# A state space layer's group loop on VectorE: six turns of a register loop against six turns of straight code

## The chip, the cores and the metric

The kernel runs on one NeuronCore of a Trainium2 chip, as one program. The time is device microseconds of one execution; a kernel is judged by the median of several runs. The engines have their names of the profile: PE is the matrix engine (PEld its weight loads), DVE is VectorE, ACT ScalarE, POOL GpSimd, SP the queue that issues most transfers; a q behind a name (DVEq) is the engine's sequencer, which runs register instructions, branches and waits and leaves the engine itself idle.

## What is computed

One inference step of a two-layer decoder: a Mamba-2 state space layer and a dilated attention layer, each between two gated feed-forward halves, for one prompt of 512 tokens and 8 samples of 8 tokens, all with the same weights. The change lies in the state space mixer:

```python
def ssd_mixer(u, conv_state, ssm_state, w_in, conv_w, conv_b, dt_bias, a_log, d_skip, norm_g, w_out):
    proj = u @ w_in
    z, xbc, dt_raw = ...
    xpad = jnp.concatenate([conv_state.astype(xbc.dtype), xbc], axis=1)
    xc = conv_b + sum(xpad[:, k:k + l] * conv_w[k] for k in range(CONV_W))
    xc = jax.nn.silu(xc)
    ...
    y, h_last = ssd_chunked(xs, dt, a, bm, cm, h0)
    y = y + d_skip.astype(f32).reshape(SSD_GROUPS, SSD_HPG)[:, :, None] * xs.astype(f32)
    gz = (y.reshape(b, l, D_INNER) * jax.nn.silu(z.astype(f32))).reshape(b, l, SSD_GROUPS, D_INNER // SSD_GROUPS)
    gz = gz * lax.rsqrt(jnp.mean(gz * gz, axis=-1, keepdims=True) + EPS)
    gz = (gz.reshape(b, l, D_INNER) * norm_g.astype(f32)).astype(u.dtype)
    return gz @ w_out, new_conv, new_ssm
```

There are 8 groups of 4 heads. A group has four tiles of 128 features to convolve with 4 taps (two of x, one of B, one of C), two tiles of the gate z, chunks of 128 tokens for the scan, and its own slice of w_in and w_out.

## The kernel before

The engines are programmed one by one, each in the order in which its code stands, and wait for each other on counting semaphores. All 576 tokens stand along the free axis, features on the 128 partitions. Products are made of a high and a low part of each factor for exactness: ACT makes the high part of a block of weights (`wh`, line 953), POOL subtracts it from the raw weights to have the low part (`wl`, line 793), PE multiplies three times.

The state space layer goes by groups. Group 0 and group 7 are written out, groups 1 to 6 are one loop body on every engine (`Fori`, with the turn's number in a register). The text calls the loop's pass for group g turn g. In turn g, DVE finishes the convolution of group g, adds the output product of group g-1 to x eight times (`back`, line 2739), does the masks, decays and states of group g, and moves the projections of group g+1 out of PSUM, PE being busy with these projections meanwhile. The start of a DVE turn is:

```python
conv(g, 2, 0)        # first tap of tile 2
back(g - 1, 0)       # x tile 0 += output product
conv(g, 2, 1)        # second and third tap
for m in range(1, 4):
    back(g - 1, m)
```

A tap is one multiply-add on 128x600 elements of SBUF (line 2710); the next tap reads what it wrote, so DVE waits for its own semaphore `dve_self` between them (`step`, with the class `Steps`, lines 132 to 154). PE's output product of tile m + 1 waits for `so_evac`, which `back` raises, since its PSUM banks are free only then. At the end of a turn DVE scales by the reciprocal root (lines 2918, 2921), adds to the four parts of the samples' state tile `h0` (line 2888, signal `ss_evac`), evacuates the gate (2719) and makes the low part of the output's factor (2929). SP stores `h0` when `ss_evac` has counted (line 650) and, next in its queue, loads the second-next block of weights (line 576), which ACT and POOL then split.

In the loop every count that depends on the turn is a value made from registers: a wait for `self.base + self.n`, `so_mm` for `g * 6 + ...`, the address of a column `cw[:, one(g * 20 + ...)]`. In straight code all of these are constants in the instruction.

Of the kernel before, what the change touches and what calls it, by code (L numbers as in the profile page):

```python
# [13 lines left out]

# [1 line left out]

# [1 line left out]

# [19 lines left out]
HEADS, GROUPS, HPG, PD, NST = 32, 8, 4, 64, 128  # L40
# [24 lines left out]
U_LOOP = U_GRP + 4  # L65
U_TAIL = U_GRP + 8 * GROUPS - 4
# [55 lines left out]
TREE_SUMMED = {0: 0, 1: 1, 3: 2}  # L122
PLAIN_U = {1: 0, 4: 1}
NORM_OF_FFN = (0, 2, 3, 5)
SSD_DVE_STEPS = 15
QKV_ORDER = (2, 5, 8, 0, 1, 3, 4, 6, 7)
AHEAD = 3
TB, TW = 6, TOK // 6
# [3 lines left out]
class Steps:  # L132
# [1 line left out]

    def __init__(self, eng, sem):
        self.eng, self.sem, self.base, self.n = eng, sem, 0, 0

    def done(self, ins):
        ins.then_inc(self.sem, 1)  # L140
        self.n += 1

    def wait(self):
        self.eng.wait_ge(self.sem, self.base + self.n)

    @contextmanager
    def loop(self, first, last, per):

        start, self.n = self.n, 0
        with self.eng.Fori(first, last) as i:  # L150
            self.base = (i - first) * per + start
            yield i
        assert self.n == per, f"{self.n} signals in a turn, not {per}"
        self.base, self.n = 0, start + (last - first) * per

def step_kernel(nc, io):
    with ExitStack() as ctx:
# [241 lines left out]
        def two(ap):  # L400

            return ap.rearrange("p (h n) -> p h n", h=2)
# [1869 lines left out]
        def _(dve):  # L2272
            self_ = Steps(dve, dve_self)
# [362 lines left out]
            def ssd():  # L2636
# [92 lines left out]
                def back(g, m):  # L2729

                    if m % 4 == 3:
                        u = U_TAIL + 2 + m // 4 if isinstance(g, int) and g == GROUPS - 1 else None
                        if u is None:
                            u = U_TAIL + m // 4 if isinstance(g, int) else (g + 1) * 8 + (U_LOOP + 3 * (m // 4))
                        dve.wait_ge(unit_done, u + 1)
                    else:
                        dve.wait_ge(so_mm, g * 6 + (m - m // 4 + 1))
                    b = 2 * (m % 2)
                    V.tensor_tensor(two(x[:, m, :]), two(x[:, m, :]), ps[:, b:b + 2, 0:HALF], ALU.add).then_inc(so_evac, 1)

                def group(g, first, last):
# [8 lines left out]
                    if not first:  # L2750
                        conv(g, 2, 0)
                        back(g - 1, 0)
                        conv(g, 2, 1)
                        for m in range(1, 4):
                            back(g - 1, m)
# [7 lines left out]
                    if last:  # L2763
                        back(g - 1, 4)
                        back(g - 1, 5)
                    else:
                        conv(g, 3)
                        if not first:
                            ahead(0)
# [186 lines left out]
                gate_in(0, 1, U_GRP + 5)  # L2956
                conv(0, 2)
                group(0, True, False)
                with self_.loop(1, GROUPS - 1, SSD_DVE_STEPS) as g:
                    group(g, False, False)  # L2960
                group(GROUPS - 1, False, True)

# [171 lines left out]
            for m in (1, 2):  # L3134
                V.tensor_tensor(sqs[:, m, :], x[:, m, :], x[:, m, :], ALU.mult)
            ffn(0, 1)
            ssd()

            ffn(1, 3)
# [176 lines left out]
```

## Time and profile before

| | us |
|---|---|
| runs | 2452.45, 2455.61, 2458.88 |
| median | 2455.61 |
| profiled execution | 2457.03 |
| its span | 2455.2 |
| PE busy | 2413.4 (98% of the span) |
| DVE busy | 1854.5 (76%) |
| ACT busy | 1394.2 (57%) |
| POOL busy | 735.9 (30%) |
| mean granted clock of PE | 0.992 of full speed |
| DVE's loop of groups 1 to 6 | 494.9 to 893.5 of the span |

Busy time is of the engine's own instructions; register instructions, branches and waits are not in it. A timeline row gives the start of an instruction and its length; brackets behind it, where there are any, give the idle time of the engine ahead of it and what ended that. A row without brackets followed the one before it with no idle time that the view shows.

### The profile page before, as it was taken

How to read it: one execution, taken by the hardware profiler on the slowest of the kernel's cores; microseconds unless marked ns; L12 is line 12 of the kernel's file. 1: busy time of each engine (PE TensorE's matmuls, PEld its weight loads, DVE VectorE, ACT ScalarE, POOL GpSimd, SP SyncE). 2: the span in 40 equal slices, each digit the busy share in tenths (PEclk: the TensorE clock that was granted, in tenths of full speed). 3: DMA queues.
4: the chain of work that ended last, by engine and by line, in shares of the span. 5: the costliest groups of instructions: out<-in, count | busy, mean ns of one | idle time of the engine just before them, and what ended most of it. 6: DMA issues, size and time to landing. Idle time of an engine off the chain costs nothing.

```text
span 2455.2 us, 50197 instructions
## 1 busy us (share of the span) xinstructions
PE 2413.4 (98%) x19713; PEld 2361.6 (96%) x19713; DVE 1854.5 (76%) x3054; ACT 1394.2 (57%) x2388; POOL 735.9 (30%) x675
## 2 busy tenths in 40 slices
PE   8999999999999999999999999999999999999998
PEld 8999999899999989999999999999999998999998
DVE  8979767978888888978876988875235438988875
ACT  7757553645555556757666767664223227767663
POOL 1222233444445532222223122224322321222222
PEclk9999999999999999999999999999999999999999
DMA  7777743123333325677765677763443334677762
GB/s 192 165 169 174 164 121 113 47 95 106 106 106 97 105 82 132 165 162 169 166 146 133 155 173 161 172 148 129 158 133 123 136 110 105 161 171 162 174 149 89
DMA packets 105686, 339.01 MB, mean 138 GB/s; under 512 B 13776, under 2 KB 17360, under 8 KB 87184
## 3 DMA queue, kind: packets, MB, share of 16 engines
q1 hardware_dynamic: 53936, 242.40, 29.9%
q0 software_dynamic: 51552, 93.87, 22.7%
q8 instruction: 137, 2.24, 0.4%
q14 instruction: 61, 0.50, 0.1%
HBM read 223.06 MB, written 19.32 MB: 99 GB/s over the span
## 4 chain that ended last, share of the span: by engine, by line
PE 90%; DVE 6%; issue 2%; ACT 1%; DMA 1%; DVEq 0%; SPq 0%; POOL 0%; POOLq 0%; ACTq 0%
PE ps L1641 17%; PE ps L1639 17%; PE ps L1649 17%; PE ps L1537 6%; PE ps L1545 6%; PE ps L1538 6%; PE ps L1658 2%; PE ps L1659 2%; PE ps L1666 2%; PE ps L1977 1%; PE ps L1979 1%; PE ps L1978 1%; PE ps L1588 1%; PE ps L1578 1%; PE ps L1579 1%
## 5 line engine op out<-in xcount | busy, mean ns | idle before, releaser
L1641 PE MATMUL ps<-sb_ual,sb_hw 128*128 128x288 f32 x2240 | 612.5, 295 | 0.0
L1639 PE MATMUL ps<-sb_uah,sb_hw 128*128 128x288 f32 x2240 | 609.1, 295 | 0.4 <-ACT sb_hr L1029 0.2
L810 POOL DMA_DIRECT2D sb_lw<-sb_rawf x328 | 283.0, 868 | 959.2 <-ACT sb_lw L984 942.5
L1639 PEld LDWEIGHTS ps<-sb_uah,sb_hw 128*128 128x128 f32 x2240 | 420.8, 188 | 1.0 <-issue 0.8
L1641 PEld LDWEIGHTS ps<-sb_ual,sb_hw 128*128 128x128 f32 x2240 | 421.1, 188 | 0.0
L793 POOL TENSOR_TENSOR sb_wl<-sb_raw,sb_wh 128x1024 fp32r<-128x1024 f32 (+1 forms) x106 | 262.3, 2475 | 410.6 <-ACT sb_wh L953 385.8
L1649 PE MATMUL ps<-sb_uah,sb_lw 128*128 128x288 f32 x2240 | 384.3, 293 | 0.6 <-DMA sb_lw<-sb_rawf 0.6
L1537 PE MATMUL ps<-sb_uh,sb_wh 128*128 128x288 f32 x1360 | 374.2, 302 | 0.7 <-DVE sb_zs L2719 0.6
L1538 PE MATMUL ps<-sb_ul,sb_wh 128*128 128x288 f32 x1360 | 367.3, 297 | 0.0
L1649 PEld LDWEIGHTS ps<-sb_uah,sb_lw 128*128 128x128 f32 x2240 | 327.9, 188 | 1.3 <-DMA sb_lw<-sb_rawf 0.8
L1537 PEld LDWEIGHTS ps<-sb_uh,sb_wh 128*128 128x128 f32 x1360 | 256.1, 188 | 8.3 <-issue 5.3
L982 ACT CAST sb_hw<-sb_rawf 128x512 fp32r<-128x512 f32 x336 | 208.3, 620 | 87.5 <-PE ps L1649 72.2
L1538 PEld LDWEIGHTS ps<-sb_ul,sb_wh 128*128 128x128 f32 x1360 | 256.2, 188 | 0.5
L1641 PE MATMUL ps<-sb_hl,sb_hw 128*128 128x288 f32 x896 | 243.9, 295 | 0.0
L1639 PE MATMUL ps<-sb_hh,sb_hw 128*128 128x288 f32 x896 | 243.3, 293 | 0.0
L953 ACT CAST sb_wh<-sb_raw 128x1024 fp32r<-128x1024 f32 (+1 forms) x106 | 111.4, 1052 | 205.2 <-PE ps L1545 127.8
L984 ACT ACTIVATE sb_lw<-sb_rawf 128x512 fp32r<-128x512 f32 x328 | 207.1, 632 | 0.0
L2338 DVE TENSOR_TENSOR sb_lw<-sb_tw,sb_hw 128x1024 fp32r<-128x1024 f32 x112 | 137.1, 1224 | 92.2 <-ACT sb_hw L1019 88.0
L1545 PE MATMUL ps<-sb_uh,sb_wl 128*128 128x288 f32 x1360 | 195.4, 296 | 0.0
L1019 ACT CAST sb_hw<-sb_tw 128x1024 fp32r<-128x1024 f32 x112 | 117.9, 1053 | 122.8 <-PE ps L1649 122.8
L1545 PEld LDWEIGHTS ps<-sb_uh,sb_wl 128*128 128x128 f32 x1360 | 186.3, 189 | 0.8 <-issue 0.6
L1641 PEld LDWEIGHTS ps<-sb_hl,sb_hw 128*128 128x128 f32 x896 | 168.4, 188 | 0.0
(366 smaller groups left out, 5115.1 us busy)
## 6 DMA issues: line engine op xcount, KB each, us to landing
sb_lw<-sb_rawf POOLq DMA_DIRECT2D x358, 256.0 KB, 3.6
sb_rawf<-w_ffn_in SPq DMA_DIRECT2D x87, 1024.0 KB, 5.1
sb_rawf<-w_ffn_so SPq DMA_DIRECT2D x32, 1024.0 KB, 5.1
sb_raw<-w_ssd SPq DMA_DIRECT2D x64, 512.0 KB, 3.6
sb_raw<-w_att SPq DMA_DIRECT2D x40, 512.0 KB, 3.9
sb_rawf<-w_ffn_out SPq DMA_DIRECT2D x32, 384.0 KB, 3.0
sb_h<-state SPq DMA_DIRECT2D x8, 1024.0 KB, 5.0
ssm_sample<-sb_h SPq DMA_DIRECT2D x8, 1024.0 KB, 4.8
```

Source lines behind the costliest of these rows:

```text
L793: pool.tensor_tensor(wl[parity][:, 0:width], raw[:, parity, 0:width], wh[parity][:, 0:width].bitcast(F32), ALU.subtract).then_inc(wl_done, 1)
L810: pool.dma_start(slot(lw, p), rawf[:, s % 2, i * BL:(i + 1) * BL], accum_op=ALU.add).then_inc(ld_in[i], 16)
L982: nc.scalar.copy(slot(hw, p), src).then_inc(hd_done, 1)
L984: nc.scalar.activation(slot(lw, p), src, ACT.Copy, scale=-1.0).then_inc(nd_done, 1)
L1019: nc.scalar.copy(slot(hw, 7, 2), tw[:, 2 * BL:4 * BL]).then_inc(ht34_done, 1)
L1537: pe.matmul(ps[:, b, 0:n], w, rh[:, k, t0:t0 + n], start=first and k == 0, stop=False)
L1538: pe.matmul(ps[:, b, 0:n], w, rl[:, k, t0:t0 + n], start=False, stop=False)
L1545: ins = pe.matmul(ps[:, b, 0:n], w, rh[:, k, t0:t0 + n], start=False, stop=last and k == nk - 1)
L1639: pe.matmul(out, w[:, k * P:(k + 1) * P], high[k], start=begins and k == 0, stop=False, skip_group_check=True)
L1641: pe.matmul(out, w[:, k * P:(k + 1) * P], low[k], start=False, stop=False, skip_group_check=True)
L1649: ins = pe.matmul(out, v[:, k * P:(k + 1) * P], high[k], start=False, stop=k == 3, skip_group_check=True)
L2338: V.tensor_tensor(slot(lw, 7, 2), tw[:, 2 * BL:4 * BL], slot(hw, 7, 2).bitcast(F32), ALU.subtract).then_inc(lt34_done, 1)
```

## The change

The DVE program alone is changed. The loop over groups 1 to 6 becomes a Python `for`, which writes six copies of the body one after the other with constants in all counts and addresses. The helper `loop` of `Steps` goes, with its base and the number of signals in a turn; `back` computes the same numbers for its waits in another form. PE, ACT, POOL and SP keep their loops with registers.

```diff
@@ class Steps
     def __init__(self, eng, sem):
-        self.eng, self.sem, self.base, self.n = eng, sem, 0, 0
+        self.eng, self.sem, self.n = eng, sem, 0
...
     def wait(self):
-        self.eng.wait_ge(self.sem, self.base + self.n)
-
-    @contextmanager
-    def loop(self, first, last, per):
-
-        start, self.n = self.n, 0
-        with self.eng.Fori(first, last) as i:
-            self.base = (i - first) * per + start
-            yield i
-        assert self.n == per, f"{self.n} signals in a turn, not {per}"
-        self.base, self.n = 0, start + (last - first) * per
+        self.eng.wait_ge(self.sem, self.n)
...
                 def back(g, m):
 
                     if m % 4 == 3:
-                        u = U_TAIL + 2 + m // 4 if isinstance(g, int) and g == GROUPS - 1 else None
-                        if u is None:
-                            u = U_TAIL + m // 4 if isinstance(g, int) else (g + 1) * 8 + (U_LOOP + 3 * (m // 4))
+                        u = (U_TAIL + 2 + m // 4 if g == GROUPS - 1 else U_TAIL + m // 4 if g == GROUPS - 2
+                             else (g + 1) * 8 + (U_LOOP + 3 * (m // 4)))
                         dve.wait_ge(unit_done, u + 1)
...
                 group(0, True, False)
-                with self_.loop(1, GROUPS - 1, SSD_DVE_STEPS) as g:
+                for g in range(1, GROUPS - 1):
                     group(g, False, False)
                 group(GROUPS - 1, False, True)
```

The listings show each engine's instructions in their order; lines of the changed kernel stand 11 or 12 lower. ISA and REGISTER_ALU are register work of the sequencer. The loop body of before has 66 such rows; in the changed kernel there are none, and DVE's listing grows from 2434 to 2759 rows. The listings of the other four engines have the same rows in the same order as before.

DVE at the start of a turn, before: the taps of tile 2 (`sb_acc`) around the first add to x.

```order
L2710 ISA [waits tap_done]
L2710 SCALAR_TENSOR_TENSOR sb_acc<-sb_xp,sb_cw,sb_acc 128x600
L144 ISA
L2737 ISA [waits dve_self]
L2739 TENSOR_TENSOR sb_x<-sb_x,ps 128x576 [waits so_mm]
L2710 ISA
L2710 SCALAR_TENSOR_TENSOR sb_acc<-sb_xp,sb_cw,sb_acc 128x600
L144 REGISTER_ALU
L2710 ISA [waits dve_self]
L2710 SCALAR_TENSOR_TENSOR sb_acc<-sb_xp,sb_cw,sb_acc 128x600
L2737 REGISTER_ALU
L2739 TENSOR_TENSOR sb_x<-sb_x,ps 128x576 [waits so_mm]
```

The same place of the changed kernel:

```order
L2699 SCALAR_TENSOR_TENSOR sb_acc<-sb_xp,sb_cw,sb_acc 128x600 [waits tap_done]
L2727 TENSOR_TENSOR sb_x<-sb_x,ps 128x576 [waits so_mm,dve_self]
L2699 SCALAR_TENSOR_TENSOR sb_acc<-sb_xp,sb_cw,sb_acc 128x600
L2699 SCALAR_TENSOR_TENSOR sb_acc<-sb_xp,sb_cw,sb_acc 128x600 [waits dve_self]
L2727 TENSOR_TENSOR sb_x<-sb_x,ps 128x576 [waits so_mm] x2
```

The engine's instructions and their waits are the same; the register rows between them are gone, and a wait that stood on a register row now stands on the instruction itself.

DVE at the normalization near the end of a turn, before: reciprocal, the two scalings (`sb_ysb`), the state update (`sb_h`).

```order
L2918 RECIPROCAL sb_gnr<-sb_gnr 128x576 [waits gz_ready,gsqrt_ready]
L144 REGISTER_ALU
L2921 REGISTER_ALU [waits dve_self]
L2921 SCALAR_TENSOR_TENSOR sb_ysb<-sb_ysb,sb_ng,sb_gnr 128x576
L2921 REGISTER_ALU
L2921 SCALAR_TENSOR_TENSOR sb_ysb<-sb_ysb,sb_ng,sb_gnr 128x576
L2887 REGISTER_ALU [waits ss_mm]
L2888 TENSOR_TENSOR sb_h<-sb_h,ps 128x512 [waits hm_done]
```

And in the changed kernel:

```order
L2906 RECIPROCAL sb_gnr<-sb_gnr 128x576 [waits gz_ready,gsqrt_ready]
L2909 SCALAR_TENSOR_TENSOR sb_ysb<-sb_ysb,sb_ng,sb_gnr 128x576 [waits dve_self]
L2909 SCALAR_TENSOR_TENSOR sb_ysb<-sb_ysb,sb_ng,sb_gnr 128x576
L2876 TENSOR_TENSOR sb_h<-sb_h,ps 128x512 [waits hm_done,ss_mm]
L2876 TENSOR_TENSOR sb_h<-sb_h,ps 128x512 [waits hm_done] x3
```

Here too the order of the engine's work stays, and the register rows behind the wait for `dve_self` are gone.

## Rows read from the trace of the kernel before

**Rows 1.** The page: its part 1, engines, and its part 4, the chain that ended last.

```profile
PE 2413.4 (98%) x19713; PEld 2361.6 (96%) x19713; DVE 1854.5 (76%) x3054; ACT 1394.2 (57%) x2388; POOL 735.9 (30%) x675
...
PE 90%; DVE 6%; issue 2%; ACT 1%; DMA 1%; DVEq 0%; SPq 0%; POOL 0%; POOLq 0%; ACTq 0%
```

**Rows 2.** Waits of PE in 494.9 to 893.5: engine, line, releaser, us, times, longest.

```profile
PE ps L1778 <- DVE sb_h L2888: 3.5, 1, 3.5
...
PE ps L1977 <- DVE sb_x L2739: 2.3, 1, 2.3
```

**Rows 3.** Chain of waits from 640 to 850: start us, us, what.

```profile
707.00 2.11 PE ps L1545 x16
...
775.84 2.13 PE ps L1545 x16
...
841.01 2.11 PE ps L1545 x16
```

**Rows 4.** Timeline of PE in turn 5: start us, us, engine, line, operation, idle before.

```profile
767.75 0.40 PE L1977 MATMUL ps<-sb_gh,sb_wh 128*128 128x288 f32 x1 [2.33 <-DVE sb_x L2739]
...
768.39 0.29 PE L1978 MATMUL ps<-sb_gl,sb_wh 128*128 128x288 f32 x1
...
768.92 0.44 PE L1978 MATMUL ps<-sb_gl,sb_wh 128*128 128x288 f32 x1
```

**Rows 5.** Timeline of DVE in turn 5, the add and the third tap.

```profile
762.42 0.75 DVE L2739 TENSOR_TENSOR sb_x<-sb_x,ps 128x576 f32<-128x576 f32 x1
...
764.07 2.97 DVE L2710 SCALAR_TENSOR_TENSOR sb_acc<-sb_xp,sb_cw,sb_acc 128x600 f32<-128x600 f32 x1
```

**Rows 6.** Timeline of POOL in turns 3, 4, 5 and the last group.

```profile
633.74 3.06 POOL L793 TENSOR_TENSOR sb_wl<-sb_raw,sb_wh 128x1024 fp32r<-128x1024 f32 x1 [4.54 <-ACT sb_wh L953]
...
698.92 2.98 POOL L793 TENSOR_TENSOR sb_wl<-sb_raw,sb_wh 128x1024 fp32r<-128x1024 f32 x1 [4.87 <-ACT sb_wh L953]
...
764.03 2.37 POOL L793 TENSOR_TENSOR sb_wl<-sb_raw,sb_wh 128x1024 fp32r<-128x1024 f32 x1 [4.45 <-ACT sb_wh L953]
...
897.87 2.37 POOL L793 TENSOR_TENSOR sb_wl<-sb_raw,sb_wh 128x1024 fp32r<-128x1024 f32 x1 [4.84 <-ACT sb_wh L953]
```

**Rows 7.** Timeline of DVE in turns 3, 4 and the last group.

```profile
633.69 0.85 DVE L2710 SCALAR_TENSOR_TENSOR sb_acc<-sb_xp,sb_cw,sb_acc 128x600 f32<-128x600 f32 x1
...
697.14 0.75 DVE L2739 TENSOR_TENSOR sb_x<-sb_x,ps 128x576 f32<-128x576 f32 x1 [0.39 <-PE ps L1979]
...
698.80 0.84 DVE L2710 SCALAR_TENSOR_TENSOR sb_acc<-sb_xp,sb_cw,sb_acc 128x600 f32<-128x600 f32 x1
...
896.34 0.75 DVE L2739 TENSOR_TENSOR sb_x<-sb_x,ps 128x576 f32<-128x576 f32 x1 [0.61 <-PE ps L1979]
...
897.88 3.00 DVE L2710 SCALAR_TENSOR_TENSOR sb_acc<-sb_xp,sb_cw,sb_acc 128x600 f32<-128x600 f32 x1
```

**Rows 8.** Timeline of DVE: reciprocal and line 2921, group 0 and turn 5.

```profile
486.73 3.74 DVE L2918 RECIPROCAL sb_gnr<-sb_gnr 128x576 f32<-128x576 f32 x1
...
490.51 2.68 DVE L2921 SCALAR_TENSOR_TENSOR sb_ysb<-sb_ysb,sb_ng,sb_gnr 128x576 f32<-128x576 f32 x1
...
817.65 3.75 DVE L2918 RECIPROCAL sb_gnr<-sb_gnr 128x576 f32<-128x576 f32 x1 [1.31 <-ACT sb_gnr L1358]
...
821.53 1.55 DVE L2921 SCALAR_TENSOR_TENSOR sb_ysb<-sb_ysb,sb_ng,sb_gnr 128x576 f32<-128x576 f32 x2
```

**Rows 9.** Line 2710 alone: engine, operation, count, ns min/median/max, first and last start.

```profile
L2710 DVEq FUSED_REGOPS  x72: 57/57/81, 495.0 to 868.1; - x72
```

**Rows 10.** Timeline of DVE, the first tap of turn 6.

```profile
830.06 0.83 DVE L2710 SCALAR_TENSOR_TENSOR sb_acc<-sb_xp,sb_cw,sb_acc 128x600 f32<-128x600 f32 x1
```

**Rows 11.** Timeline of DVE, the last state update of turn 4.

```profile
755.89 0.68 DVE L2888 TENSOR_TENSOR sb_h<-sb_h,ps 128x512 f32<-128x512 f32 x1
```

**Rows 12.** Timeline of SP, the transfer of the weights that follow.

```profile
757.37 0.35 SPq L576 DMA_DIRECT2D sb_raw<-w_ssd  x1
```

**Rows 13.** Waits of DVE in 494.9 to 893.5.

```profile
DVE sb_x L2739 <- PE ps L1979: 23.6, 34, 2.0
```

More of the change, by code:

```diff
@@ L17 @@
-from contextlib import ExitStack, contextmanager
+from contextlib import ExitStack
 import numpy as np
@@ L124 @@
 NORM_OF_FFN = (0, 2, 3, 5)
-SSD_DVE_STEPS = 15
 QKV_ORDER = (2, 5, 8, 0, 1, 3, 4, 6, 7)
```

## The prediction

> **What bounds the kernel now.** I read the page first: the matmul engine PE is busy 98% of the span and carries 90% of the chain that ended last [rows 1]. An edit on VectorE (DVE) can therefore pay only where PE waits for it. The loop of groups 1 to 6 lies between 494.9 and 893.5 us. The waits of PE in that stretch are two only: 3.5 us at its entrance and 2.3 us at line 1977 [rows 2]. The first has its cause in group 0, which is straight code already. It ends with the update of the state tile (line 2888) of group 0, which comes late since the scaling at line 2921 ran from 490.51 for 2.68 us. The later pair of the same operation took 1.55 us for both [rows 8]. The change does not touch that. So at most the second wait is to be had, and I looked at what it costs. In the chain of waits the same sixteen matmuls of the next group begin at 707.00, 775.84 and 841.01 [rows 3]: periods of 68.84 and 65.17 us. 
>
> **Why turn 5 and no other.** PE at 767.75 waits for an output tile to be added to x (line 2739), and that add stands behind the third tap of the convolution of tile 2 (line 2710, the second half of conv(g, 2)). This tap took 2.97 us in turn 5, from 764.07, and 0.84 us in the others [rows 5, 7]. GpSimd (POOL) started its subtraction of the low weights (line 793) at 764.03 [rows 6], 0.04 us ahead of it; it ends at 766.40, and the tap right after. In turn 3 the tap began at 633.69 and the subtraction at 633.74 [rows 6, 7]; there the tap took its 0.85 us, and the subtraction 3.06 us instead of 2.37. So these two shut each other out: whichever starts first keeps its pace, the other waits to its end. The tap is first by 0.05 us in turn 3 and 0.12 in turn 4; the rows of turns 2 and 6 read the same, with leads between these. It loses by 0.04 in turn 5, and by 0.01 in the last group, outside the loop [rows 5 to 7]. Only a tap that loses stops PE.
>
> The Trainium skill says this of the hardware: SBUF — State Buffer, section Who interferes with whom, has the port pair of the two engines as an exclusive lock, given by issue order, for the whole instruction. The trace agrees with it in both orders, as just read. By a shared bandwidth instead, 0.1 us of lead would be worth about 0.1 us a turn and the change nothing.
>
> **The change, part by part.** *The register work goes.* A turn of the loop has 66 register rows in the listing of DVE, the two of the loop's end among them; 72 of one line take 57 ns each [rows 9]. Most run while the engine is busy. They cost where DVE waits for its own last result and only then computes the next address. There the listing shows one ahead of each tap. From the start of the add at 697.14 to the third tap at 698.80 are 1.66 us in turn 4; the same three instructions in the last group, straight code, take from 896.34 to 897.88, 1.54 us [rows 7]. So a tap comes 0.11 or 0.12 us earlier after the add; I take 0.11. The add itself cannot come earlier than PE's output (line 1979): in turn 4 it waited 0.39 us for it. In turn 5 it did not wait, 762.42, while PE's event by the period of 65.1 us was due at 697.14 + 65.1 = 762.3; without the register rows in front of it the add comes at about 762.3.
>
> *What else moves.* The rival of the tap starts when its weights have landed, and SP issues that transfer at 757.37, behind a store that waits for the end of DVE's state update (line 2888, the last from 755.89 for 0.68 us) [rows 11, 12]. From the end of that update to POOL's start are 764.03 - 756.57 = 7.46 us. So POOL moves with DVE. Ahead of that update lies one gap with register work in it: from the reciprocal (817.65 + 3.75) to line 2921 at 821.53 are 0.13 us in the loop; in group 0 from 486.73 + 3.74 to 490.51 they are 0.04 [rows 8]. POOL comes 0.09 us earlier. The start of the reciprocal hangs on ScalarE and PE (idle 1.31 us before it) and stays.
>
> *The race after the change*, turn 5: tap at 762.3 + 1.54 = 763.84, POOL at 764.03 - 0.09 = 763.94. The tap leads by 0.10. In the others the lead changes by +0.11 - 0.09 where the add waits for PE: turn 4, 0.14. In turn 3 PE's event was due at 697.14 - 65.1 = 632.0; with it the tap comes at 633.54 and POOL at 633.65, a lead of 0.11. Turns 2 and 6 lie between. The last group was straight before; its POOL comes 0.09 earlier as well, so it loses by 0.10 and keeps its stall. Worth: -3.7 us in turn 5, 0 elsewhere.
>
> *The other DVE gaps* (some 0.1 us each, at the taps, the state recurrence and line 2726) end in waits for PE: 23.6 us for line 1979 alone over the six turns [rows 13]. They cost nothing now and give nothing. Bounds for all of it: 0, and the 57 ns of 66 rows in six turns, 22.6 us, were DVE the bound. With that waiting left on DVE, and PE idle in two places only, I take 0.
>
> *The end of the loop.* The trace shows no pause there: the first tap of turn 6, at 830.06, has no idle time ahead of it [rows 10]. Nothing is won. The Trainium skill, Runtime: NRT & Kernel Launch, section Instruction fetch mechanics, says that a taken branch to a page no longer held must wait for a fetch, which is why kernels prefer full unrolling. The trace does not agree for this loop: no idle time at its end, so by measurement this is worth 0 and not a fetch per turn.
>
> *The code grows* by five turns. A fetch that is late is not in this trace, so bounds: below, one register instruction's 57 ns won in each turn, 0.3 us; above, a stall as long as that of turn 5, 2.1 us on DVE in each of the five added turns. That would cost PE something only where it hits the stretch between 829 and 833 or its like. The straight last group, with the same instructions, shows no idle time but for PE. I take 0.
>
> **Sum.** The profiled execution took 2457.03 us (span 2455.2 and 1.8 around it). 2457.03 - 3.7 = 2453.3. It lies 1.4 us above the median shown, 2455.61; the three runs are 3.2 us apart each, about the size of one such stall, so a run seems to lose this race a varying number of times, and I set 2453.3 as the time, 0.1% under the median.
>
> **Rivals.**
> 1. *The race stays open.* Leads of 0.09 to 0.14 us are won against a landing whose delay differs between turns: POOL waited 4.45 us for its weights in turn 5 and 4.87 in turn 4 [rows 6]. One turn loses as before: 2457.0. For it: the tap lost by 0.04 only. Against: both sides hang on the same chain of DVE and PE, and the new leads are double the old.
> 2. *POOL wins (slower).* The state update moves earlier than the tap does. It decides from 0.2 us on: if POOL came 0.2 us earlier instead of 0.09, the leads of all five turns from 2 to 6 would be gone, as in the last group, where SP and POOL are out of their loops too. Five turns lost instead of one: 2457.0 + 4 x 3.7 = 2471.8; three lost: 2464.4. Against: between reciprocal and update I find the one gap.
> 3. *The last group too.* If its landing is late by 0.1 us, its tap wins, and PE's idle time behind it goes too: 2453.3 - 3.7 = 2449.6. Against: it goes the wrong way by the 0.09.
> 4. *DVE was the bound*, hidden behind matmuls whose ends are modelled: up to 22.6 us less; with half of it 2445.7. Against: a period of 65.1 us in every undisturbed turn, whether or not DVE stalled elsewhere in it.
> 5. *Nothing comes of it*, with other collisions of these two engines shifted by 0.1 us: counted with rival 1, the same time.
>
> **Chances.** Forecast 0.60, rival 1 (with 5) 0.23, rival 2 0.07, rival 3 0.07, rival 4 0.03. Changes of under 0.3% (7.4 us) can hardly be told from none with this kernel. Faster than 2448.2 needs rival 4 or rival 3 with luck: 0.05. Slower than 2463.0 needs rival 2 with three turns or more: 0.06. Within: 0.89. The range takes in rivals 1 and 3 and a microsecond or two of scatter as between the runs before: 2449.5 to 2459.0.
>
> **What would show it.** In the profile after: no register instructions on DVE; 1.54 us from add to third tap in each turn; the tap at 0.84 us in turns 2 to 6, and each of POOL's subtractions beside it near 3.0 us, not 2.37; the reciprocal's end to line 2921 in 0.04 us; no wait of PE for line 2739 in the loop; periods of 65.1 us throughout; the stall of the last group still there, and the 3.5 us at the loop's entrance. I am wrong in the mechanism if a turn has 65.1 us although its tap lost, or if PE's turns become shorter than 65.1; in the step on POOL if the time from the state update to its start is no longer near 7.46 us.

## The result, and the profile after

The changed kernel takes 2468.95 us (median of 16 runs, 2455.86 to 2473.39), the kernel before on the same chip 2459.45 us (median of 16, 2452.45 to 2464.76). The ratio is 1.003 with a 95% interval of 1.0019 to 1.0041: slower by 0.2 to 0.4%. The forecast was 2453.3 us in a range of 2449.5 to 2459.0, a change too small to be told from none. The profiled execution took 2461.54 us (span 2459.7), against 2457.03 before.

The page of the kernel after, its parts 1 and 4, reads almost as that of before [rows 1]:

```profile
PE 2412.9 (98%) x19713; PEld 2359.7 (96%) x19713; DVE 1865.0 (76%) x3054; ACT 1393.0 (57%) x2388; POOL 732.0 (30%) x675
...
PE 91%; DVE 6%; ACT 1%; issue 1%; DMA 0%; SPq 0%; POOL 0%; DVEq 0%; ACTq 0%
```

DVE is busy 10.5 us longer, with the same 3054 instructions. Some 6.6 us of that are three more taps that took 3.0 us instead of 0.84: time in which it is shut out. Three instructions of line 2817 (2829 before) also take some 2 us longer each, in turns 2, 3 and 6. PE does not wait for these: its periods there (below) are longer by the wait behind the tap alone. The waits of PE between 490 and 930 us say where it stands still (engine, tile, line, releaser: us in all, times, longest). This window takes in the last group, which that of [rows 2] leaves out:

```profile
PE ps L1966 <- DVE sb_x L2727: 10.9, 5, 2.2
PE ps L1767 <- DVE sb_h L2876: 3.6, 1, 3.6
```

Line 1966 is the old 1977, 2727 the old 2739, 2699 the old 2710. The one stall of the loop has become four, and the last group kept its own. In the chain of waits the same sixteen matmuls in turns 2 to 6 are these, where [rows 3] shows three of them (start us, us, what):

```profile
579.47 2.11 PE ps L1534 x16
...
646.75 2.11 PE ps L1534 x16
...
711.82 2.11 PE ps L1534 x16
...
780.61 2.12 PE ps L1534 x16
...
847.91 2.11 PE ps L1534 x16
```

The periods are 67.28, 65.07, 68.79 and 67.30 us. Only the second, with turn 4's tap in it, is undisturbed. The timelines of DVE and of POOL in turn 5, which answer to [rows 5] and [rows 6]:

```profile
767.13 0.76 DVE L2727 TENSOR_TENSOR sb_x<-sb_x,ps 128x576 f32<-128x576 f32 x1 [0.19 <-PE ps L1968]
767.80 3.91 DVE L2699 SCALAR_TENSOR_TENSOR sb_acc<-sb_xp,sb_cw,sb_acc 128x600 f32<-128x600 f32 x2
```

```profile
768.70 2.37 POOL L782 TENSOR_TENSOR sb_wl<-sb_raw,sb_wh 128x1024 fp32r<-128x1024 f32 x1 [4.47 <-ACT sb_wh L942]
```

The row of DVE holds two taps. The first keeps its 0.88 us to the next start, so the third started at 768.68 and ran 3.03 us. POOL started 0.02 us *behind* it and yet kept its 2.37 us. The turn was lost with the tap in front. Turns 2, 3 and 6 read the same, with leads of the tap of 0.03, 0.00 and 0.03 us (a lead is the time from the start of the third tap to the start of POOL's low weights). Turn 4 has a lead of 0.05 (its third tap starts at 703.61) and is won: both taps together take 1.72 us, and POOL is the one that is long.

```profile
702.06 0.76 DVE L2727 TENSOR_TENSOR sb_x<-sb_x,ps 128x576 f32<-128x576 f32 x1 [0.21 <-PE ps L1968]
702.74 1.72 DVE L2699 SCALAR_TENSOR_TENSOR sb_acc<-sb_xp,sb_cw,sb_acc 128x600 f32<-128x600 f32 x2
```

```profile
703.66 3.05 POOL L782 TENSOR_TENSOR sb_wl<-sb_raw,sb_wh 128x1024 fp32r<-128x1024 f32 x1 [4.51 <-ACT sb_wh L942]
```

**Why the leads are small.** The add waits for PE's last matmul of the tile (line 1968, line 1979 before). The timeline of PE, first of the kernel after in turn 5, then of the kernel before in turn 4:

```profile
766.73 0.30 PE L1968 MATMUL ps<-sb_gh,sb_wl 128*128 128x288 f32 x1
```

```profile
696.81 0.30 PE L1979 MATMUL ps<-sb_gh,sb_wl 128*128 128x288 f32 x1
```

It ends at 767.03 after, and the add starts at 767.13, 0.10 us later. It ended at 697.11 before, and the add started at 697.14 [rows 7], 0.03 us later. So in straight code the add itself reacts 0.07 us more slowly to the same event. What DVE's sequencer does at that add's waits (line, engine, operation, count in the whole program, ns min/median/max, first and last start), first in the kernel after, then in the kernel before:

```profile
L2725 DVEq EVENT_SEMAPHORE  x7: 21/21/21, 502.4 to 903.1; - x7
```

```profile
L2737 DVEq FUSED_REGOPS  x6: 53/53/53, 499.8 to 830.9; - x6
L2737 DVEq EVENT_SEMAPHORE  x1: 21/21/21, 896.3 to 896.3; - x1
```

The add has to wait twice: for the first tap of DVE itself and for PE. In the loop one register instruction of line 2737 stood between tap and add in each turn (53 ns, six of them for six turns), and the wait for the tap sat on it; the add carried PE's alone. In straight code nothing stands there. A semaphore instruction of its own takes one of the two waits, seven times after, and before only in the last group.

The register instruction had a price of its own when the tap ahead ended late. In turn 5 before, the first tap ended at 762.28, behind PE's last matmul, and the add started 0.14 us after the tap, 0.20 behind PE:

```profile
761.45 0.83 DVE L2710 SCALAR_TENSOR_TENSOR sb_acc<-sb_xp,sb_cw,sb_acc 128x600 f32<-128x600 f32 x1
```

This is how the loop lost that turn. In the kernel after the add is 0.11 us behind PE in every turn, also in turn 6, where the first tap ended with PE's matmul: the change made the latest add earlier and all the others later.

### The profile page after: what moved, and what is told of

It is laid out like the page before. It is cut to its first block, busy times and chain, and to the rows that moved or that the text cites. A ratio compares the mean times of both kernels' runs of the same rounds, so it can differ in the third digit from the quotient of the medians.

```text
span 2459.7 us, 49830 instructions
## 1 busy us (share of the span) xinstructions
PE 2412.9 (98%) x19713; PEld 2359.7 (96%) x19713; DVE 1865.0 (76%) x3054; ACT 1393.0 (57%) x2388; POOL 732.0 (30%) x675
## 4 chain that ended last, share of the span: by engine, by line
PE 91%; DVE 6%; ACT 1%; issue 1%; DMA 0%; SPq 0%; POOL 0%; DVEq 0%; ACTq 0%
PE ps L1630 17%; PE ps L1628 16%; PE ps L1638 16%; PE ps L1526 7%; PE ps L1534 7%; PE ps L1527 7%; PE ps L1647 2%; PE ps L1648 2%; PE ps L1655 2%; PE ps L1966 1%; PE ps L1968 1%; PE ps L1967 1%; DVE sb_acc L2699 1%; PE ps L1577 1%; PE ps L1567 1%; PE ps L1568 1%
```

## The experiments

Each group of kernels that ran together shared its runs of the kernel before.

**1. flat_free_add.** The second wait is taken off the add, and stands on the next tap:

```diff
-                        if t < CONV - 1:
+                        if part == 0 and k == 2:
+                            self_.done(ins)
+                        elif t < CONV - 1:
...
                         back(g - 1, 0)
+                        self_.wait()
                         conv(g, 2, 1)
```

> The changed kernel, with DVE's wait for its own first tap put behind the add to x that follows instead of ahead of it (the add doesn't read the tap). Race theory: the add then begins when PE's output is there, at 5.76 us behind the state update instead of 5.84, the third tap at 7.30, POOL at 7.41 to 7.43: a lead of 0.11 or more, the tap wins in turns 2 to 6; the last group, whose add already waits for PE, still loses. 8 to 13 us less than the changed kernel, ratio to before 0.997 to 1.000. Fetch theory: as the changed kernel, 1.003.

Measured: 2454.98 us, 0.9987 of before (0.9978 to 0.9996). Straight as the change, and yet faster than before. The timelines of PE, DVE and POOL in turn 5:

```profile
763.10 0.30 PE L1968 MATMUL ps<-sb_gh,sb_wl 128*128 128x288 f32 x1
```

```profile
763.43 0.76 DVE L2729 TENSOR_TENSOR sb_x<-sb_x,ps 128x576 f32<-128x576 f32 x1 [0.19 <-PE ps L1968]
764.11 1.72 DVE L2699 SCALAR_TENSOR_TENSOR sb_acc<-sb_xp,sb_cw,sb_acc 128x600 f32<-128x600 f32 x2
```

```profile
765.10 2.98 POOL L782 TENSOR_TENSOR sb_wl<-sb_raw,sb_wh 128x1024 fp32r<-128x1024 f32 x1 [4.56 <-ACT sb_wh L942]
```

The add comes 0.03 us behind PE again, the leads are 0.08 to 0.12 us in turns 2 to 6 and 0.10 in the last group, and no tap is lost. These are nearly the leads that the prediction gave (0.10 to 0.14). One wait moved by one instruction is the whole difference to the changed kernel. The last group had been expected to lose, and that it won is owed in part to chance: POOL started there 7.46 us behind the end of the state updates, against 7.26 to 7.29 in the profiles of the kernels before and after. With the same edit on the loop (experiment 7) it was 7.28, and the tap lost.

**2. flat_pool_late.** The changed kernel, with POOL made late instead: `pool.tensor_tensor(spare[:, 0:1], masks[:, 0:1], masks[:, 1:2], ALU.subtract)` in front of its first low weights of each turn.

> The changed kernel (straight code on DVE), with one tiny subtraction of POOL (128x1) ahead of its first low-weights subtraction of each turn, so that POOL comes some 0.1 to 0.2 us later to the third tap. Race theory (the tap lost in four turns of five because it leads by only 0.00 to 0.03 us): the leads become 0.1 us and more, the tap takes 0.84 us in turns 2 to 6 and perhaps in the last group too (it loses there by 0.06), PE has no 2.2 us wait in the loop; 10 to 15 us less than the changed kernel, some 2 to 8 us less than the kernel before: ratio to before 0.997 to 0.999. Fetch theory (straight code costs DVE or PE instruction loads): nothing in the code's length changes, ratio to before stays 1.003 to 1.004.

Measured: 2455.61 us, 0.9986 (0.9977 to 0.9995). The leads are 0.14 to 0.86 us in the loop, nothing is lost there, and 0.02 in the last group, which is lost. So the add may stay late, if only POOL is later. A lead of 0.85 us is the tap's whole length: there the tiny subtraction itself was shut out, and took up to 0.82 us instead of 0.19, after which the large one met no tap at all. POOL in turn 5 of flat_free_late (experiment 8), where the tap began at 768.35:

```profile
768.45 0.79 POOL L783 TENSOR_TENSOR sb_spare<-sb_masks 128x1 f32<-128x1 f32 x1 [4.76 <-ACT sb_wh L944]
769.20 2.39 POOL L784 TENSOR_TENSOR sb_wl<-sb_raw,sb_wh 128x1024 fp32r<-128x1024 f32 x1
```

**3. flat_reorder.** The changed kernel, with the adds that PE waits for ahead of the third tap: tap 1, add 0, tap 2, add 1, tap 3, add 2, add 3 (conv is cut into three parts for it).

```diff
                         back(g - 1, 0)
                         conv(g, 2, 1)
+                        back(g - 1, 1)
+                        conv(g, 2, 2)
-                        for m in range(1, 4):
+                        for m in range(2, 4):
```

> The changed kernel, with the second add to x moved ahead of the third tap (tap, add, tap, add, tap, add, add). The add reads PSUM and one tile of SBUF and was never held by POOL. Race theory: POOL now always starts before the third tap and holds it for up to 2.4 us in every turn, but PE needs only the second add at that time, so its 2.2 us waits for line 2739 go in all turns and in the last group: 12 to 18 us less than the changed kernel, ratio to before 0.995 to 0.998. If a held tap cost by itself (DVE behind for the rest of the turn), nothing would be won: 1.003. Fetch theory: 1.003 too.

Measured: 2456.10 us, 0.9988 (0.9979 to 0.9997), short of the 0.995 to 0.998 expected. The third tap is held in every turn, as here in turn 5, and costs PE no 2.2 us, since the add that PE waits for is already done:

```profile
765.92 2.36 DVE L2699 SCALAR_TENSOR_TENSOR sb_acc<-sb_xp,sb_cw,sb_acc 128x600 f32<-128x600 f32 x1
```

No wait of line 1966 for the add is left, but each turn pays some: periods of 65.29 to 65.33 us, since PE now waits elsewhere:

```profile
PE ps L1526 <- DVE sb_x L2727: 2.6, 6, 0.5
```

**4. loop_tap_late.** From the other side, the loop of before made to lose by a later third tap: `V.tensor_copy(spare[:, 0:1], masks[:, 0:1])` in front of it.

> The kernel before, loop and registers kept, with one tiny copy of DVE (128x1) ahead of the third tap, so that the tap comes some 0.1 us later. Race theory: the leads of 0.05 to 0.12 us are used up, the tap loses in most of turns 2 to 6, and each loss costs 2.2 us, or 3.7 us where the granted clock falls after it: 6 to 14 us more than the kernel before, ratio 1.002 to 1.006, as slow as straight code without being straight. Fetch theory: ratio 1.000.

Measured: 2457.49 us, 1.0001 (0.9991 to 1.0010). The expectation failed, since the tap was hardly delayed: from add to tap are 1.66 us instead of 1.65, the register work in front of the tap having run beside the copy. Leads 0.08 to 0.14 us in turns 2 to 6, none lost in the loop. It tells nothing of the race but that leads of this size win.

**5. loop_tap_later.** The same with three copies.

> The kernel before, loop kept, with three tiny copies of DVE (128x1) ahead of the third tap. One copy had moved the tap by 0.01 us only, since the register work ran beside it; three should move it by 0.15 to 0.25. Race theory: the leads of 0.05 to 0.12 us turn negative, the tap loses in all of turns 2 to 6, each at 2.2 us or, where the granted clock falls, 3.7: 8 to 16 us more than the kernel before, ratio 1.003 to 1.006. Fetch theory: ratio 1.000.

Measured: 2469.28 us, 1.0038 (1.0021 to 1.0055), as slow as the changed kernel, with the loop kept. So the loss needs no straight code. From add to tap 1.74 us; leads in turns 2 to 6 0.01, -0.03, 0.03, -0.02 and 0.00; four of these lost, and the last group. Its waits of PE:

```profile
PE ps L1977 <- DVE sb_x L2742: 11.4, 5, 2.3
```

It has the one turn in all profiles that was won with a lead under 0.04 us, turn 4. DVE and POOL there:

```profile
706.66 0.83 DVE L2713 SCALAR_TENSOR_TENSOR sb_acc<-sb_xp,sb_cw,sb_acc 128x600 f32<-128x600 f32 x1
```

```profile
706.68 3.06 POOL L793 TENSOR_TENSOR sb_wl<-sb_raw,sb_wh 128x1024 fp32r<-128x1024 f32 x1 [4.64 <-ACT sb_wh L953]
```

**6. flat_again.** The changed kernel once more, for a second profile.

> The changed kernel itself once more, beside the others of this call on one chip. Both theories: ratio to before 1.002 to 1.004. Race theory: three to five of turns 2 to 6 lose the third tap, with leads of 0.00 to 0.05 us, the add to x starts 0.11 us after the end of PE's last product for it (0.04 in the loop), and each lost turn shows one PE wait of 2.2 us.

Measured: 2464.34 us, 1.0019 (1.0007 to 1.0031). Leads 0.03, 0.05, 0.01, 0.01 and 0.04 us in turns 2 to 6. Again only the 0.05 is won; it is in turn 3 here, not in turn 4. The add is 0.11 us behind PE throughout. From the matmuls behind the output product in turn 1 to the same in the last group, six periods with all these races in them, 404.3 us pass, as in the first profile of this kernel (404.4), and against 398.1 and 397.2 in the two profiles of the kernel before. That its span is 10.7 us longer (2470.4) comes from elsewhere in the program.

**7. loop_free_add.** The edit of flat_free_add on the loop.

> The kernel before, loop kept, with DVE's wait for its own first tap put behind the first add to x. Race theory: turns in which the first tap ended late (as turn 5 before) now begin the add as soon as PE is done, 0.04 us after it; leads 0.09 to 0.12 in all five turns, none lost; the last group, straight code, gets its add 0.07 us earlier and wins about every second time. 3 to 6 us less than before, ratio 0.998 to 0.999, the same as straight code with the same edit (0.9987): then straight code by itself is worth less than 1 us. If straight code itself were worth something, or cost something, the two would differ.

Measured: 2459.39 us, 1.0002 (0.9991 to 1.0013). The profile is as expected in the loop (leads 0.07 to 0.10 us, all won, periods 65.11 to 65.17), and the last group was lost with 0.02. The time is not: it should have won 3.7 us wherever the kernel before loses a turn. Expected were 0.998 to 0.999. Either that kernel mostly loses none in runs without a profile, or the scatter hid it. This stays open.

**8. flat_free_late.** Both remedies on the changed kernel, **and 9. flat_late_again,** the same word for word beside its twin below.

> Both edits on the changed kernel: the wait for its own first tap behind the add, and POOL's tiny subtraction ahead of its large one. Race theory: leads of 0.2 us and more, no tap lost in any turn or the last group, in all runs: as the single edits or up to 2 us less, ratio 0.998 to 0.9987, with less scatter between runs. If the runs scatter as before, the scatter has another cause than this race.

> flat_free_late word for word, beside its loop twin. Both theories: ratio to the kernel before 0.998 to 0.999 as at its first run (0.9985), no third tap lost, periods of 64.9 to 65.05 us. Race theory: 0.0002 to 0.0003 under loop_free_late, which a timing of five rounds can hardly tell; rival: 0.0008 or more above it.

Measured: 2454.87 us, 0.9985 (0.9976 to 0.9994), then 2454.97 us, 0.9983 (0.9974 to 0.9993). Nothing lost, leads 0.19 to 0.86 us. Its runs still spread over 9 to 10 us, so most of the scatter is not the race. Some of it may be: the runs of the kernels that lose four or five taps in a profile spread over 18 us (the change), 13 (flat_again) and 20 (loop_tap_later).

**10. loop_free_late.** Both remedies on the loop of before. With the race out of both (here too no tap is lost, with leads of 0.18 to 1.24 us), this pair is the change by itself.

> Kernel before (turns as a loop) with both edits: the wait for DVE's own first tap stands behind the add, and POOL does one 128x1 subtraction ahead of its first low weights of each turn. The race is then out in the loop too, and what is left between this kernel and its straight twin flat_late_again is the worth of straight code by itself. Race theory: leads of 0.8 us or more in every turn and the last group, third tap 0.84 us, no PE idle at line 1977's place; periods of 65.10 to 65.15 us against 65.00 to 65.03 of the twin, so the twin is faster by 6 x 0.1 = 0.6 us, 0.0002 to 0.0003; ratio to the kernel before 0.998 to 0.999. Rival (straight code costs something outside this race, late instruction fetches for instance): this kernel is faster than its twin by 2 us or more.

Measured: 2454.03 us, 0.9978 (0.9966 to 0.9991); the straight twin 0.9983. The two can't be told apart. The straight twin's median is 0.9 us higher, and with twelve runs each, spread over 8 to 9 us, the true difference may be anything from 1 us in its favour to 3 us against it (an estimate from that spread). So the timing makes the rival, late instruction fetches of 2 us or more, unlikely and does not exclude it; the two profiles show no sign of it, the straight one being the shorter by 1.7 us (2453.2 against 2454.9). In the chain of waits straight code does have its 0.1 us a turn. First the loop, then the straight twin, the two sixteens around turn 5's output row:

```profile
760.85 2.13 PE ps L1547 x16
775.80 2.11 PE ps L1547 x16
```

```profile
759.29 2.11 PE ps L1536 x16
774.10 2.11 PE ps L1536 x16
```

14.95 us against 14.81. The periods are 65.11 to 65.17 against 64.99 to 65.05 us.

**11. flat_states_first.** flat_free_late, and in group 0 the state updates that the 3.5 us wait at the loop's entrance hangs on go ahead of the scalings:

```diff
+                    if first:
+                        sample_states(range(4))
                     for i in range(2):
                         V.scalar_tensor_tensor(two(ysb[:, i, :]), two(ysb[:, i, :]), ng[:, one(g * 2 + i)], inverse,
...
-                        sample_states(range(4))
+                        if not first:
+                            sample_states(range(4))
```

> flat_free_late, and in group 0 alone DVE does the four state updates ahead of the two scalings, not behind them. In flat_free_late the updates of group 0 come behind 3.4 us of scalings and PE waits 3.5 us for them at the entrance of turn 1, with a fall of the clock. If that wait ends last there: it goes, 3.5 us and up to 1.4 us of clock less, ratio 0.9985 - 0.0014 to 0.0020 = 0.9965 to 0.9971. Rival: the scalings come 2.5 us later, PE's next wait is for the output row (the halves of the gated row) instead, and the time stays at 0.9985 or gets longer by 1 to 2 us.

Measured: 2452.18 us, 0.9976 (0.9965 to 0.9986), the fastest of all, though not certainly faster than its parent (0.9983), and short of what was expected. Its waits of PE:

```profile
PE ps L1968 <- DVE sb_x L2731: 2.0, 1, 2.0
PE ps L1968 <- DVE sb_gl L2925: 1.5, 1, 1.5
```

The wait of 3.5 us went; 1.5 us came back at the output row, for the reason of the rival, and 2.0 us since everything in turn 1 had moved, and its third tap, which had never been near POOL, now met it with a lead of -0.02 us and took 2.99 us.

**12. before_again.** The kernel before, for a second profile.

> The kernel before word for word, for a second profile of it. Race theory: the add 0.03 to 0.05 us behind PE's event, leads of -0.05 to 0.13 us in turns 2 to 6, each turn with a lead of 0.04 us or less lost and each with 0.05 or more won, so none to two lost, and the last group lost. Rival (the order is settled by something else than these leads): turns lost at leads over 0.06.

Measured: 2458.06 us. Leads 0.01, 0.09, 0.12, 0.10 and 0.05 us in turns 2 to 6. Turn 2 is lost, the others won. DVE and POOL in turn 2:

```profile
569.46 4.01 DVE L2710 SCALAR_TENSOR_TENSOR sb_acc<-sb_xp,sb_cw,sb_acc 128x600 f32<-128x600 f32 x2
```

```profile
570.45 2.38 POOL L793 TENSOR_TENSOR sb_wl<-sb_raw,sb_wh 128x1024 fp32r<-128x1024 f32 x1 [4.51 <-ACT sb_wh L953]
```

Here the third tap begins at 570.44. So turn 5 was nothing special: the loop loses about one turn, now this, now that.

**All meetings together.** In the eleven profiles whose DVE has no copies and the old order there are 77 pairs of a third tap and low weights, the wide leads of turn 1 counted. The 17 lost taps have leads from -0.10 to 0.035 us; the 60 won have 0.048 us or more. In 29 of the 60 the low weights start only when the tap has ended, mostly because the tiny subtraction was shut out in their place, so 31 won taps were contested by them. With loop_tap_late and loop_tap_later it is 91 pairs and the one exception above; the lost leads go down to -0.22 there. That exception stands behind a copy that was still running when the tap started; whether this is why it won was not tested.

## Why the prediction was wrong

- **"So a tap comes 0.11 or 0.12 us earlier after the add; I take 0.11": right.** 1.54 to 1.55 us in every turn after, and 1.65 before.
- **"POOL comes 0.09 us earlier": right in its cause, too small as a size.** From the reciprocal's end to the end of the state updates are 3.97 us after and 4.06 before. From there to POOL are 7.41 to 7.43 after and 7.42 to 7.46 before: the 7.46 given was the longest of five. Against PE's last matmul of the tile, POOL starts 1.65 to 1.70 us behind it after and 1.78 to 1.82 before, so it comes 0.11 to 0.14 earlier. The gap between reciprocal and scaling is 0.04 us in turn 5 of the kernel after, where [rows 8] had 0.13; its timeline of DVE:

```profile
753.56 3.75 DVE L2906 RECIPROCAL sb_gnr<-sb_gnr 128x576 f32<-128x576 f32 x1 [1.30 <-ACT sb_gnr L1347]
757.35 1.54 DVE L2909 SCALAR_TENSOR_TENSOR sb_ysb<-sb_ysb,sb_ng,sb_gnr 128x576 f32<-128x576 f32 x2
```

- **"Without the register rows in front of it the add comes at about 762.3", at PE's event: wrong, and this step failed.** The add comes 0.10 to 0.11 us behind PE, not 0.03 to 0.04. The prediction took register instructions for pure cost; one of them carried a wait, which now stands with another on the add and costs 0.07 us more there. Removing this one wait (flat_free_add) gives back nearly the leads forecast, the won taps and the time. The sum of a turn whose add waits for PE is +0.11 for the tap, -0.11 for POOL, -0.07 for the add: in turns 2, 4 and 6 the lead shrinks by 0.07, from 0.10 to 0.03 in the mean, where it was to grow by 0.02. The leads forecast were 0.11, 0.14 and 0.10 in turns 3, 4 and 5; measured are 0.00, 0.05 and 0.02. In turn 5 the 762.3 itself was nearly right, by luck: it is 0.09 us behind PE's last matmul, put at PE's event by a round period, and two thirds of the miss there are POOL's.
```profile
572.50:576.00 3.50, 3.18 (x21) 1.00 0.52 150
...
772.40:776.00 3.60, 3.57 (x13) 0.53 0.40 139
```

- **The rival that came true is the second, by its place and its count** (three turns lost 2464.4, five 2471.8; in both profiles four were lost, and 2468.95 measured), **but not by its mechanism**: it had POOL 0.2 us earlier, and POOL came 0.11 to 0.14 earlier, the add doing the rest. Its chance was 0.07, far too little for a race whose known leads were about as large as the moves under discussion. Three turns more than before at 2.2 to 3.7 us are 6.6 to 11 us; the ratio says 4.7 to 10.
- **"I am wrong in the mechanism if PE's turns become shorter than 65.1":** they did, by 0.1 us, in the straight kernels without losses (64.99 to 65.05 us in flat_late_again). The prediction took 0 for the other gaps of DVE. It is 0.6 us in all; which gap it is, no run here shows. By the prediction's own sign this is a miss of the mechanism as well, though not the one that made the kernel slower.
- **The fetch: right as far as shown.** The twins (loop_free_late against flat_late_again) give no sign of 2 us or more that hang on the longer code. The Trainium skill (Runtime: NRT & Kernel Launch, section Instruction fetch mechanics) has kernels prefer full unrolling where possible; here the twin with its loop is as fast. Its reason is a branch to a page that is no longer held, and no run shows whether this loop's start ever was such a page, so the prediction's "the trace does not agree" says more than the trace can.
- **The last group kept its stall, the entrance its wait (3.6 us, 3.5 before): right.**

## What to carry to other kernels

Where two engines contend for a lock and a third waits for the outcome, write down the lead as a sum of both paths, and ask of every instruction that goes, register work too, which wait it carried and where that wait goes now. A lead of a few hundredths of a microsecond is no lead: give the engine on the path 0.1 us or more (take a wait off it, or make its rival late by a tiny instruction), and it held in both forms of the code here. Straight code that stands beside the loop in the same program, as the last group does here, is a sample of what unrolling will do: its add came 0.11 us behind PE before anything was changed, and the trace had that to be read.

## What the hardware showed that was not expected

- A second wait on an instruction of DVE costs 0.07 us from the event to the start (0.10 to 0.11 against 0.03 to 0.04 us), with a 21 ns semaphore instruction in front.
- The lock between DVE and POOL goes to POOL up to a lead of the tap of 0.035 us, and to the tap from 0.048 us, in 90 of 91 pairs, in 30 of which the two did not overlap.
- An idle time of PE of 2.2 us was followed by a fall of the granted clock to the lower level in some turns (idle from 770 and 906 us) and not in others (571, 638, 839 us) of one execution, the changed kernel's, and so costs 3.7 or 2.2 us. What decides between them was not tested.
- A small copy on DVE (128x1) delayed the next instruction by only 0.01 us where register work stood between them: the two ran side by side. Three copies cost 0.08 us.
